# Attention scores in three PSUM banks with the context part shared, router results in the mixer bank, value products in three pieces

## The chip, the core and the metric

The program runs on one core of one Trainium2 chip. The time is that of the device, in microseconds (us), for one execution of the whole program. The engines of the core work in parallel, each through its own queue in order, and wait for each other through semaphores: TensorE (PE in the profile), VectorE (DVE), ScalarE (ACT), GpSimd (POOL) and SyncE (SP), which here only issues DMAs.

## What is computed

One layer of a hybrid backbone over 2048 tokens of width 1024, with 256 context tokens. The change lies in the part behind the input projection: windowed attention, the mixing of its rows with those of the Hyena branch, the output projection, the residual and the router. From the reference, cut:

```python
def block(i):                      # 16 blocks of 128 queries, 8 heads on 2 key heads
    qb = q[q0:q0+128]; kb = k_pad[q0:q0+384]; vb = v_pad[q0:q0+384]
    s_band = einsum('bqkgd,bskd->bkgqs', qb, kb) * ATT_SCALE     # 384 local keys, masked
    s_ctx  = einsum('bqkgd,bckd->bkgqc', qb, kc) * ATT_SCALE     # 256 context keys
    p = softmax(concatenate([s_sink, s_ctx, s_band], axis=-1))
    return p_ctx @ vc + p_band @ vb
...
mix = concatenate([rms_norm(att), rms_norm(hy)], axis=-1) @ w_out
x = x + g1 * mix
h = modulate(rms_norm(x, norm2_w), sh2, sc2)
# router: softmax over 4 groups, top 1; over its 8 experts, top 2; tokens sorted by expert
x = x + g2 * hierarchical_moe(h, ...)
```

## The kernel before

The program is a row of stages. Stages 1 to 4 make the modulation, the projection, the keys, queries and values, and the Hyena branch; stage 6 runs the experts. The change is in stage 5 (`stage5`), with one load in the stage ahead of it. Stage 5 goes over 16 tiles of 128 tokens (`NT = 16`) in a software pipeline (`pipeline`), steps -1 to 18. Step n of each engine's code holds five pieces of work, each for another tile:

- `scores`, tile n+1 (called `nx`): for each of 8 heads, TensorE multiplies the queries with the 256 context keys and the 384 local keys into PSUM. VectorE adds the mask, writes the sum to `pr` and takes the maximum, all in one instruction (`L2127`), then makes the bias (`L2131`). ScalarE takes the exponential (`L2040`).
- `values`, tile n: TensorE turns the exponentials by transposes (`L1932`, five groups of four for four heads, ten in all, into two alternating banks `PT`), ScalarE copies them out (`L2034`), TensorE multiplies them with the values into `OT` (`tile_values`, `L1956`, two halves of 10 products), turns the result (`turn_values`), and VectorE scales it into `mix`.
- `project`, tile n-1 (`pj`): TensorE transposes the normalised mixer rows into the two banks of `M` (`L1998`, semaphore `t1`), ScalarE and VectorE split them into a high and a low part (`L2087`, `L2213`, semaphore `t1v`), TensorE multiplies with `w_out` in two halves (`project_half`, `L1970` to `L1972`, 48 passes), VectorE adds the residual.
- `route`, tile n-2 (`ro`): ScalarE squares the new rows (`L2064`, semaphore `sq2`), GpSimd inverts the root (`n2d`), VectorE normalises them (`L2185`, `xnd`), TensorE transposes them into `M` (`L1980`, `t2`), VectorE and ScalarE scale them into `h2T` (`L2192`, `L2079`; `t2v`, `t2a`), TensorE makes the router's logits (`L2006`), VectorE picks group and experts in a chain of small instructions.
- `place`, tile n-3 (`pl`): GpSimd makes the one-hot picks (`L1860` to `L1863`, semaphore `picked`), TensorE sums them over the tokens (`L1988`, `L1989`), VectorE reads the sums (`L2207`), GpSimd works out the slots and scatters the records.

No scheduler sets the order: each engine's `step` is written out by hand, and the heads (`head(p)`) are the slots between which the other pieces stand. GpSimd's step begins with the wait for `sq2` of tile n-2, makes `n2d`, and only then makes the picks of tile n-3. SyncE's step n loads the queries of tile n+1 (`L1790`), waits for the normalised mixer rows and loads the Hyena rows of tile n+1 into `mix` (`L1796`), then loads the residual rows (`L1799`) and stores two results (`L1806`, `L1808`), each behind its wait. It goes to step n+1 only when it is through.

The eight PSUM banks are: `S` two (one head's scores, 640 columns, lie across both), `PT` two, `OT` one, `M` two, `R` one (router logits and pick sums). So the products of a head wait until VectorE has read those of the head before (semaphore `sm`); for tiles 0 and 1 odd heads use `M` and don't wait. The two products of a head use the two halves of TensorE's rows: the context keys rows 64 to 127, the local keys rows 0 to 63.

Of the kernel before, what the change touches and what calls it, by code (L numbers as in the profile page):

```python
# [1184 lines left out]
def stage4(e, g):  # L1185
# [24 lines left out]
    with e.stage() as st:  # L1210
# [50 lines left out]
        def _(sp):  # L1261
# [55 lines left out]
            sp.dma_start(g.mask[:, :, :], i["mask"].rearrange("p (a k) -> p a k", a=3)).then_inc(ld_att, 16)  # L1317
# [4 lines left out]
            sp.wait_ge(ld_att, 16 * 5)  # L1322
# [317 lines left out]
def stage5(e, g):  # L1640
# [3 lines left out]
    with e.stage() as st:  # L1644
# [3 lines left out]
        woh = e.sb(st, "woh", [P, KT, D], F32R)  # L1648
        rw = e.sb(st, "rw", [P, KT, NG + NE])
        rb = e.sb(st, "rb", [P, NG + NE])  # L1650
        g1 = e.sb(st, "g1row", [P, D])
        mask, sink = g.mask, g.sink
        e.sb(st, "mask_room", [P, 3, KEYS])
        e.sb(st, "sink_room", [P, NH])
        e.sb(st, "qb0_room", [2 * HD, NH, P])
# [19 lines left out]
        mixn = e.sb(st, "mixn", [P, 2, HW])  # L1675
# [18 lines left out]
        S = e.ps(st, "S", [P, 2 * 512])  # L1694
# [3 lines left out]
        R = e.ps(st, "R", [P, 512])  # L1698
# [68 lines left out]
        def score_banks(tile, p):  # L1767
            if tile.n < 2 and p % 2:
                return M[:, :, :].rearrange("p a b -> p (a b)")
            return S  # L1770

        @block.sync
        def _(sp):
            def step(t, scores, values, project, route, place):
# [9 lines left out]
                if scores:  # L1784
# [7 lines left out]
                    wait(sp, mxn, b.n - 1)  # L1792
                    if isinstance(b.n, int) and b.n == 0:
# [122 lines left out]
        def _(pe):  # L1916
            pe.wait_ge(setup, 6)

            def step(t, scores, values, project, route, place):
                nx, pj, ro, pl = t.back(-1), t.back(1), t.back(2), t.back(3)  # L1920

                def head(p):
# [12 lines left out]
                    if scores:  # L1935
                        if p == 0 and nx.n:
                            pe.wait_ge(ld_q[nx.par], 32 * (nx.half + nx.par))
                        wait(pe, sm, 8 * nx.n + p - (1 if nx.n < 2 and p >= 1 else 0))
                        h = order[p]
                        kv = h // 4  # L1940
                        to = score_banks(nx, p)
                        pe.matmul(to[:, 512 - C:512], qb[nx.par][HD:2 * HD, h, :], g.kT[HD:2 * HD, kv, 0:C],  # L1942
                                  start=True, stop=True)
                        pe.matmul(to[:, 512:512 + 3 * P], qb[nx.par][0:HD, h, :],  # L1944
                                  g.kT[0:HD, kv, bass.ds(nx.n * P, 3 * P)], start=True, stop=True).then_inc(qk, 1)

                def tile_values(half):
# [3 lines left out]
                    for a in range(5):  # L1951
                        for kv in range(2):
                            v = g.v[:, a, kv * HD:(kv + 1) * HD] if a < 2 else \
                                g.v[:, t.n + a, kv * HD:(kv + 1) * HD]
# [3 lines left out]
                    ins.then_inc(pv, 1)  # L1958
# [16 lines left out]
                for p in range(4):  # L1975
                    head(p)
                if route:
# [5 lines left out]
                if values:  # L1983
                    tile_values(0)
                head(4)
                if place:
                    pe.wait_ge(picked, pl.n + 1)
                    pe.matmul(R[:, 64:64 + NE], upper[:, :], pick[:, pl.par, 2, :], start=True, stop=True)  # L1988
                    pe.matmul(R[:, 128:128 + NE], ones[:, :].broadcast_to([P, P]), pick[:, pl.par, 2, :], start=True, stop=True).then_inc(px, 1)  # L1989
                for p in range(5, 7):  # L1990
                    head(p)
                if route:
                    pe.wait_ge(t2v, ro.n + 1)
                    pe.wait_ge(t2a, ro.n + 1)
                if project:
                    pe.wait_ge(mxn, pj.n + 1)
                    for k in range(KT):
                        ins = pe.transpose(M[:, k // 4, (k % 4) * P:(k % 4 + 1) * P],  # L1998
                                           mixn[:, k // 4, (k % 4) * P:(k % 4 + 1) * P], g.ident[:, :])
                    ins.then_inc(t1, 1)  # L2000
                head(7)
                if route:
                    if place:
                        pe.wait_ge(pxr, pl.n + 1)
                    for k in range(KT):
                        ins = pe.matmul(R[:, 0:NG + NE], h2T[:, k, :], rw[:, k, :], start=(k == 0), stop=(k == KT - 1))  # L2006
                    ins.then_inc(rt, 1)
# [15 lines left out]
        def _(act):  # L2023
            def step(t, scores, values, project, route, place):
# [71 lines left out]
                if values:  # L2096
# [4 lines left out]
                    act.activation(mixn[:, 0, :], mix[t.par][:, 0, :], ACT.Square, accum_out=ms[:, t.par, 0:1])  # L2101
                    act.activation(mixn[:, 1, :], mix[t.par][:, 1, :], ACT.Square, accum_out=ms[:, t.par, 1:2]).then_inc(sqa, 1)
# [3 lines left out]
        def _(ve):  # L2106
# [10 lines left out]
            def step(t, scores, values, project, route, place):  # L2117
                nx, pj, ro, pl = t.back(-1), t.back(1), t.back(2), t.back(3)

                def head(p):  # L2120
                    if scores:
                        edge = 1
                        if isinstance(nx.n, int):
# [3 lines left out]
                        ve.tensor_tensor_reduce(out=pr[:, p, :], in0=score_banks(nx, p)[:, 512 - C:512 + 3 * P],  # L2127
                                                in1=mask[:, edge, :], scale=1.0, scalar=-3e38, op0=ALU.add, op1=ALU.max,
# [52 lines left out]
                for p in range(3):  # L2181
                    head(p)
# [12 lines left out]
                if place:  # L2195
                    ve.wait_ge(px, pl.n + 1)
                    wait(ve, rec_ok, pl.n)
                if place and pl.n == NT - 1:
                    ve.wait_ge(based, 1)
                    ve.sem_inc(passed, 1)  # L2200
                    ve.tensor_copy(pxs[:, 1, :], R[:, 128:128 + NE]).then_inc(pxr, 1)
                    do(ve.tensor_tensor(pxs[:, 0, :], R[:, 64:64 + NE], base[:, :], ALU.add))
                    do(ve.tensor_tensor(pos[:, :, :], pick[:, pl.par, 0:2, :], pxs[:, 0:1, :].broadcast_to([P, 2, NE]), ALU.mult))
                    do(ve.tensor_reduce(out=selg[:, 0, 0:2], in_=pos[:, :, :], axis=AX.X, op=ALU.add))
                    ve.tensor_copy(idx[:, pl.par, :], selg[:, 0, 0:2]).then_inc(placed, 1)
                elif place:
                    ve.tensor_copy(pxs[:, :, :], R[:, 64:192].rearrange("p (a b) -> p a b", a=2)[:, :, 0:NE]).then_inc(pxr, 1)  # L2207
                head(5)
                head(6)
# [6 lines left out]
                if route:  # L2216
                    ve.wait_ge(rt, ro.n + 1)
                    wait(ve, rec_ok, ro.n - 1)
                    ve.tensor_tensor(lg[:, ro.par, :], R[:, 0:NG + NE], rb[:, :], ALU.add).then_inc(lgd, 1)
# [9 lines left out]
                if values:  # L2229
# [5 lines left out]
                    ve.wait_ge(ott, t.n + 1)  # L2235
                    ve.tensor_tensor(mix[t.par][:, 0, :].rearrange("p (k h d) -> p h k d", k=2, h=4),
# [584 lines left out]
```

## Time and profile before

| | us |
|---|---|
| median of 3 runs | 2511.38 |
| the runs | 2505.14, 2511.58, 2511.38 |
| the profiled execution | 2501.89 |
| its span | 2500.1 |
| TensorE busy in it | 2243.6 (90%) |
| VectorE, ScalarE, GpSimd busy | 1340.5, 1148.8, 504.6 |
| stage 5 in it | from about 1001 to about 1627 |

The profile page cuts the span into 40 slices with the busy tenths of each engine and the granted clock of TensorE. Slices 17 to 25 are the steady part of stage 5, in which one step follows the other at the same distance. The timeline gives each instruction with its start, its duration and, in brackets, how long its engine was idle before it and who released it. Matmuls are pipelined, so the duration of one includes its way through the array; the distance of two starts is what it costs.

### The profile page before, as it was taken

What the parts mean: (1) busy time and instruction counts of PE and PEld (TensorE: products, weight loads), DVE (VectorE), ACT (ScalarE), POOL (GpSimd) and SP (SyncE); (2) the same over time, 40 slices, a digit from 0 to 9 for tenths busy, and PEclk for the clock granted to TensorE, in tenths of its full rate; (3) what the DMA queues carried; (4) which work ended last, traced back from release to release, by engine and by line L of the source; (5) the groups of instructions that cost most, each with busy time, mean ns of one, the idle gap of its engine ahead of it and who ended that gap; (6) DMA issues with size and microseconds to landing.
All of it is one profiled execution on the core that took longest, in us unless ns stands there. A gap on an engine that the chain in (4) does not pass through costs nothing. (4 is left out here: it accounts for less than half of the span.)

```text
span 2500.1 us, 42870 instructions
## 1 busy us (share of the span) xinstructions
PE 2243.6 (90%) x15061; PEld 1535.7 (61%) x15062; DVE 1340.5 (54%) x2309; ACT 1148.8 (46%) x2065; POOL 504.6 (20%) x842
## 2 busy tenths in 40 slices
PE   5998999999989997799999999669899999898996
PEld 2336777888756665366666666546566666556664
DVE  4556784233245554555555554347556756455763
ACT  4666221222234442644554454146556656455653
POOL 2771110000011100002222222321222122222111
PEclk8999999999989998899999999679999999999999
DMA  8993223223473533421222121649888997777993
GB/s 305 310 259 95 55 55 97 61 58 92 106 184 88 139 88 95 124 68 52 72 77 72 47 73 56 217 158 318 281 264 290 332 318 246 244 231 248 334 305 103
DMA packets 241312, 413.61 MB, mean 165 GB/s; under 512 B 25555, under 2 KB 128859, under 8 KB 236115
## 3 DMA queue, kind: packets, MB, share of 16 engines
q1 hardware_dynamic: 197248, 353.84, 43.2%
q0 software_dynamic: 18800, 44.71, 7.7%
q10 hardware_dynamic: 25125, 13.18, 1.9%
q8 instruction: 90, 1.47, 0.3%
q14 instruction: 49, 0.40, 0.1%
HBM read 344.44 MB, written 76.85 MB: 169 GB/s over the span
## 5 line engine op out<-in xcount | busy, mean ns | idle before, releaser
L936 PE MATMUL ps_proj<-sb_hTh,sb_winh 128*128 128x512 f32 x576 | 234.0, 406 | 5.1 <-DVE sb_hTl L1088 2.4
L2692 PE MATMUL ps_byp<-sb_w,sb_gT 128*128 128x512 f32 x512 | 232.8, 597 | 1.1 <-ACT sb_gT L2499 1.1
L938 PE MATMUL ps_proj<-sb_hTh,sb_winl 128*128 128x512 f32 x576 | 225.0, 391 | 0.0
L937 PE MATMUL ps_proj<-sb_hTl,sb_winh 128*128 128x512 f32 x576 | 224.7, 390 | 0.0
L2127 DVE CUSTOM_DVE_ANT_0 sb_lead<-ps_S,sb_mask 128x640 f32<-128x640 f32 x120 | 98.7, 822 | 118.4 <-PE ps_S L1944 118.0
L2692 PEld LDWEIGHTS ps_byp<-sb_w,sb_gT 128*128 128x128 f32 x512 | 92.1, 190 | 94.7 <-issue 91.8
L2040 ACT ACTIVATE sb_lead<-sb_lead,sb_nm 128x640 f32<-128x640 f32 x128 | 106.2, 830 | 84.7 <-DVE sb_nm L2131 84.0
L2034 ACT COPY sb_lead<-ps_PT 128x512 f32<-128x512 f32 x160 | 89.3, 580 | 89.7 <-PE ps_PT L1932 89.7
L936 PEld LDWEIGHTS ps_proj<-sb_hTh,sb_winh 128*128 128x128 f32 x576 | 108.6, 189 | 33.4 <-issue 4.1
L1061 ACT COPY sb_rope_or_conv<-ps_proj 128x512 f32<-128x512 f32 x48 | 28.3, 589 | 219.1 <-PE ps_proj L938 144.6
L937 PEld LDWEIGHTS ps_proj<-sb_hTl,sb_winh 128*128 128x128 f32 x576 | 108.7, 189 | 25.6 <-issue 4.1
L938 PEld LDWEIGHTS ps_proj<-sb_hTh,sb_winl 128*128 128x128 f32 x576 | 108.4, 188 | 23.3
L1942 PE MATMUL ps_S<-sb_kT,sb_qb 64*128 64x256 f32 x240 | 85.4, 436 | 40.6 <-DVE sb_mx L2127 35.3
L2406 DVE TENSOR_TENSOR sb_w1l<-sb_raw,sb_w1h 128x1024 fp32r<-128x1024 f32 x64 | 74.1, 1220 | 87.5 <-ACT sb_w1h L2469 87.5
L2406 DVE TENSOR_TENSOR sb_w1l<-sb_lead,sb_w1h 128x1024 fp32r<-128x1024 f32 x64 | 74.0, 1220 | 84.2 <-ACT sb_w1h L2469 84.2
L2681 PE MATMUL ps_bh<-sb_w1h,sb_bxh 128*128 128x512 f32 x256 | 109.2, 426 | 8.7 <-DVE sb_bxl L2420 8.7
L1562 DVE TENSOR_TENSOR sb_ab<-sb_ab,ps_gp 128x1024 f32<-128x1024 f32 x64 | 75.3, 1218 | 70.9 <-PE ps_gp L1369 70.9
L1944 PE MATMUL ps_S<-sb_kT,sb_qb 64*128 64x384 f32 x240 | 111.6, 546 | 0.0
L2501 ACT ACTIVATE sb_sg<-ps_bh 128x512 f32<-128x512 f32 x32 | 19.2, 600 | 187.2 <-PE ps_bh L2681 181.0
L1970 PE MATMUL ps_M<-sb_woh,sb_mixh 128*128 128x512 f32 x256 | 104.9, 410 | 0.0
L1144 DVE TENSOR_SCALAR sb_rope_or_conv<-sb_rope_or_conv,sb_cols 128x2048 f32<-128x2048 f32 x11 | 14.8, 1346 | 163.8 <-ACT sb_rope_or_conv L1061 163.8
L1932 PEld LDWEIGHTS ps_PT<-sb_ident,sb_lead 128*128 128x128 f32 x640 | 71.1, 143 | 49.8 <-issue 44.7
(335 smaller groups left out, 5443.2 us busy)
## 6 DMA issues: line engine op xcount, KB each, us to landing
sb_lead<-in_exp_w SPq DMA_DIRECT2D x32, 2048.0 KB, 11.7
sb_w<-in_exp_w SPq DMA_DIRECT2D x32, 2048.0 KB, 9.0
sb_raw<-in_exp_w SPq DMA_DIRECT2D x32, 2048.0 KB, 12.1
sb_ada<-in_ada_w SPq DMA_DIRECT2D x16, 1536.0 KB, 7.7
scr_filt<-sb_fout SPq DMA_DIRECT2D x128, 128.0 KB, 3.3
sb_yh<-scr_filt SPq DMA_DIRECT2D x64, 256.0 KB, 5.1
scr_hy_in<-sb_hcT ACTq DMA_DIRECT2D x12, 1024.0 KB, 5.5
sb_win<-in_w_in SPq DMA_DIRECT2D x9, 1024.0 KB
```

Of the source, the lines that this page charges most:

```text
L936: pe.matmul(mp[:, r % 4, 0:N], a, high[:, k, :], start=(k == 0), stop=False)
L937: pe.matmul(mp[:, r % 4, 0:N], a, low[:, k, :], start=False, stop=False)
L938: ins = pe.matmul(mp[:, r % 4, 0:N], b, high[:, k, :], start=False, stop=(k == KT - 1))
L1942: pe.matmul(to[:, 512 - C:512], qb[nx.par][HD:2 * HD, h, :], g.kT[HD:2 * HD, kv, 0:C], start=True, stop=True)
L1944: pe.matmul(to[:, 512:512 + 3 * P], qb[nx.par][0:HD, h, :], g.kT[0:HD, kv, bass.ds(nx.n * P, 3 * P)], start=True, stop=True).then_inc(qk, 1)
L1970: pe.matmul(M[:, half, :], mixh[:, k, :], woh[:, k, cs], start=(k == 0), stop=False)
L2034: act.copy(pt[:, 4 * c:4 * c + 4, :].rearrange("p a t -> p (a t)"), PT[:, (t.par + c) % 2, :])\
L2040: act.activation(pr[:, p, :], pr[:, p, :], ACT.Exp, bias=nm[:, nx.par, p:p + 1], scale=SCALE, accum_out=rsum[:, nx.par, p:p + 1]).then_inc ...
L2127: ve.tensor_tensor_reduce(out=pr[:, p, :], in0=score_banks(nx, p)[:, 512 - C:512 + 3 * P], in1=mask[:, edge, :], scale=1.0, scalar=-3e38, ...
L2406: ve.tensor_tensor(piece(low[m], part), piece(raw13[par][:, m], part), piece(high[m], part).bitcast(F32), ALU.subtract).then_inc(lo[m], 1)
L2681: ins = pe.matmul(hp[:, m, :], a[:, k, :], b[m][:, k, :], start=(k == 0 and j == 0), stop=(k == KT - 1 and j == 2))
L2692: ins = pe.matmul(yp[:, part, :], gT[:, f, :], w2[par][:, f, part * 512:(part + 1) * 512], start=(f == 0), stop=(f == FT - 1), skip_group_ ...
```

## The change

1. `S` has three banks. An even head's local scores lie at the end of bank 0 and an odd head's at the start of bank 2; bank 1 holds the context scores of both, even ones in its first half, odd ones in its second. So each head's 640 columns are still in one piece, but local keys come first for even heads. The mask has 256 columns more, so that both orders can be cut from it, and is loaded in two DMAs; the value products take the chunks in the matching order.
2. TensorE's head p now issues the context product of head p, which alone raises `qk`, and behind it the local product of head p+1. Head 7 issues the local product of head 0 of the next tile, behind a wait for that tile's queries. Only tile 0 still uses `M` for odd heads.
3. `R` is now the first 128 columns of the second bank of `M`. The pick sums move on TensorE from behind head 4 to behind head 1, with waits for `picked` and for the residual `res`; their reading by VectorE moves from behind head 4 to behind head 1. The router's product moves from behind head 7 to ahead of head 6, VectorE's copy of the logits from behind head 7 to behind head 5, and TensorE waits for it (`lgd`) before it transposes the mixer rows.
4. The first half of the value products is cut in three: two chunks ahead of head 4, two behind it, the last behind head 6.
5. `mixn` is gone. The mixer rows are normalised in place in `mix`, and the squares go to `h2T`, behind a wait for `rt`. SyncE's load of the Hyena rows into `mix` therefore waits for `t1` (the transposes have read the rows) and stands at the end of its step.

The heart of the diff:

```diff
+            mask_of = [slice(C, KEYS + C), slice(0, KEYS)]
...
+            scores_of = [S[:, 512 - 3 * P:512 + C], S[:, 1024 - C:1024 + 3 * P]]
+            local_of = [S[:, 512 - 3 * P:512], S[:, 1024:1024 + 3 * P]]
+            context_of = [S[:, 512:512 + C], S[:, 1024 - C:1024]]
...
 (SyncE)
-                    wait(sp, mxn, b.n - 1)
...
-                    sp.dma_start(mix[b.par][:, 1, :], g.hyo_dram[bass.ds(b.n * P, P), :]).then_inc(ld_h[b.par], 16)
...
                     sp.wait_ge(xnd, b.n + 1)
                     sp.dma_start(g.xn_dram[bass.ds(b.n * P, P), :], xn[b.par][:, :]).then_inc(st_x[b.par], 16)
+                if scores:
+                    b = t.back(-1)
+                    wait(sp, t1, b.n - 1)
+                    sp.dma_start(mix[b.par][:, 1, :], g.hyo_dram[bass.ds(b.n * P, P), :]).then_inc(ld_h[b.par], 16)
...
 (TensorE)
+                def local(tile, p):
+                    if p == 0 and tile.n:
+                        pe.wait_ge(ld_q[tile.par], 32 * (tile.half + tile.par))
+                    return pe.matmul(mixer_local if tile.n == 0 and p % 2 else local_of[p % 2], qb[tile.par][0:HD, order[p], :],
+                                     g.kT[0:HD, order[p] // 4, bass.ds(tile.n * P, 3 * P)], start=True, stop=True)
...
+                        context.then_inc(qk, 1)
+                        if p + 1 == NH and nx.n + 1 < NT:
+                            wait(pe, sm, 8 * nx.n + p)
+                            local(nx.back(-1), 0)
+                        elif p + 1 < NH and not alone:
+                            local(nx, p + 1)
...
-                for p in range(4):
+                for p in range(2):
                     head(p)
+                if place:
+                    pe.wait_ge(picked, pl.n + 1)
+                    if route:
+                        pe.wait_ge(res, ro.n + 1)
+                    pe.matmul(R[:, 64:64 + NE], upper[:, :], pick[:, pl.par, 2, :], start=True, stop=True)
+                    pe.matmul(R[:, 96:96 + NE], ones[:, :].broadcast_to([P, P]), pick[:, pl.par, 2, :], start=True, stop=True).then_inc(px, 1)
+                for p in range(2, 4):
+                    head(p)
+                if place:
+                    pe.wait_ge(pxr, pl.n + 1)
...
                 if route:
                     pe.wait_ge(t2v, ro.n + 1)
                     pe.wait_ge(t2a, ro.n + 1)
+                    for k in range(KT):
+                        ins = pe.matmul(R[:, 0:NG + NE], h2T[:, k, :], rw[:, k, :], start=(k == 0), stop=(k == KT - 1))
+                    ins.then_inc(rt, 1)
...
                 if project:
+                    if route:
+                        pe.wait_ge(lgd, ro.n + 1)
                     pe.wait_ge(mxn, pj.n + 1)
```

How the instructions stand now. First TensorE in a steady step, before, from head 1 to the first values product (`ps_PT` is the turned exponentials, `ps_S` the scores, 256 columns for the context and 384 local):

```order
L1932 MATMUL ps_PT<-sb_ident,sb_lead 128x128 x4
L1942 MATMUL ps_S<-sb_kT,sb_qb 128x256
L1944 MATMUL ps_S<-sb_kT,sb_qb 128x384
L1932 MATMUL ps_PT<-sb_ident,sb_lead 128x128 x4
L1942 MATMUL ps_S<-sb_kT,sb_qb 128x256
L1944 MATMUL ps_S<-sb_kT,sb_qb 128x384
L1932 MATMUL ps_PT<-sb_ident,sb_lead 128x128 x4
L1942 MATMUL ps_S<-sb_kT,sb_qb 128x256
L1944 MATMUL ps_S<-sb_kT,sb_qb 128x384
L1980 MATMUL ps_M<-sb_ident,sb_xn_1 128x128 x8
L1956 MATMUL ps_OT<-sb_lead,sb_v 64x256 x10
```

The same engine and place after the change, where `L1948` is the context product of a head and `L1929` the local one of the next:

```order
L1948 MATMUL ps_S<-sb_kT,sb_qb 128x256
L1929 MATMUL ps_S<-sb_kT,sb_qb 128x384
L1994 MATMUL ps_M<-sb_pick,sb_upper 128x32
L1995 MATMUL ps_M<-sb_pick,sb_ones 128x32
L1942 MATMUL ps_PT<-sb_ident,sb_lead 128x128 x4
L1948 MATMUL ps_S<-sb_kT,sb_qb 128x256
L1929 MATMUL ps_S<-sb_kT,sb_qb 128x384
L1942 MATMUL ps_PT<-sb_ident,sb_lead 128x128 x4
L1948 MATMUL ps_S<-sb_kT,sb_qb 128x256
L1929 MATMUL ps_S<-sb_kT,sb_qb 128x384
L2003 MATMUL ps_M<-sb_ident,sb_xn_0 128x128 x8
L1968 MATMUL ps_OT<-sb_lead,sb_v 64x256 x4
```

The pick sums now stand between head 1 and head 2, and only four of the ten products of the first values half stand behind the transposes. Then TensorE at the end of the heads, before:

```order
L1998 MATMUL ps_M<-sb_ident,sb_mixn 128x128 x8
L1932 MATMUL ps_PT<-sb_ident,sb_lead 128x128 x4
L1942 MATMUL ps_S<-sb_kT,sb_qb 128x256
L1944 MATMUL ps_S<-sb_kT,sb_qb 128x384
L2006 MATMUL ps_R<-sb_rw,sb_h2T 128x36 x8
L1956 MATMUL ps_OT<-sb_lead,sb_v 64x256 x10
L1970 MATMUL ps_M<-sb_woh,sb_mixh 128x512
```

And after, where the last `L1929` is that of the next tile:

```order
L2016 MATMUL ps_M<-sb_rw,sb_h2T 128x36 x8
L1942 MATMUL ps_PT<-sb_ident,sb_lead 128x128 x4
L1948 MATMUL ps_S<-sb_kT,sb_qb 128x256
L1929 MATMUL ps_S<-sb_kT,sb_qb 128x384
L1968 MATMUL ps_OT<-sb_lead,sb_v 64x256 x2
L2028 MATMUL ps_M<-sb_ident,sb_mix 128x128 x8
L1942 MATMUL ps_PT<-sb_ident,sb_lead 128x128 x4
L1948 MATMUL ps_S<-sb_kT,sb_qb 128x256
L1929 MATMUL ps_S<-sb_kT,sb_qb 128x384
L1968 MATMUL ps_OT<-sb_lead,sb_v 64x256 x10
L1983 MATMUL ps_M<-sb_woh,sb_mixh 128x512
```

The router's product went ahead of the mixer's transposes. Last SyncE's queue, one round of it, before:

```order
L1808 DMA scr_xn<-sb_xn_0 128x1024
L1790 DMA sb_qb<-scr_q 64x1024 x2
L1796 DMA sb_mix<-scr_hy_out 128x512
L1799 DMA sb_xres<-in_x 128x1024
L1806 DMA out<-sb_x_1 128x1024
```

And after:

```order
L1808 DMA scr_xn<-sb_xn_0 128x1024
L1812 DMA sb_mix<-scr_hy_out 128x512
L1792 DMA sb_qb<-scr_q 64x1024 x2
L1799 DMA sb_xres<-in_x 128x1024
L1806 DMA out<-sb_x_1 128x1024
```

The load of the Hyena rows, which waits for `t1`, now stands ahead of the two loads of queries.

## Rows read from the trace of the kernel before

**Rows 1.** The page: span, and granted clock of TensorE in 40 slices

```profile
span 2500.1 us, 42870 instructions
...
PEclk8999999999989998899999999679999999999999
```

**Rows 2.** Timeline of TensorE in step 8: start, duration, line, output from inputs, idle

```profile
1294.05 0.48 PE L1942 MATMUL ps_S<-sb_kT,sb_qb 64*128 64x256 f32 x1
...
1296.04 0.48 PE L1942 MATMUL ps_S<-sb_kT,sb_qb 64*128 64x256 f32 x1 [0.49 <-DVE sb_mx L2127]
...
1296.36 0.38 PE L1942 MATMUL ps_S<-sb_kT,sb_qb 64*128 64x256 f32 x1
1296.47 0.48 PE L1944 MATMUL ps_S<-sb_kT,sb_qb 64*128 64x384 f32 x1
1296.89 0.66 PE L1932 MATMUL ps_PT<-sb_ident,sb_lead 128*128 128x128 f32 x4
...
1300.94 1.09 PE L1980 MATMUL ps_M<-sb_ident,sb_xn 128*128 128x128 f32 x8
...
1305.29 0.48 PE L1942 MATMUL ps_S<-sb_kT,sb_qb 64*128 64x256 f32 x1
...
1310.53 1.09 PE L1998 MATMUL ps_M<-sb_ident,sb_mixn 128*128 128x128 f32 x8
...
1312.83 1.98 PE L2006 MATMUL ps_R<-sb_rw,sb_h2T 128*128 128x36 f32 x16
1314.74 2.38 PE L1956 MATMUL ps_OT<-sb_lead,sb_v 128*64 128x256 f32 x20
1317.05 0.51 PE L1970 MATMUL ps_M<-sb_woh,sb_mixh 128*128 128x512 f32 x1
```

**Rows 3.** Timeline of VectorE, step 8, head 0

```profile
1295.15 0.82 DVE L2127 CUSTOM_DVE_ANT_0 sb_lead<-ps_S,sb_mask 128x640 f32<-128x640 f32 x1 [0.35 <-PE ps_S L1944]
```

**Rows 4.** Waits from 1044 to 1550: us in total, times, longest

```profile
PE ps_S L1942 <- DVE sb_mx L2127: 34.5, 56, 1.8
```

**Rows 5.** Timeline of GpSimd, step 8: root of the norm, and last pick instruction

```profile
1296.18 0.19 POOL L1846 TENSOR_SCALAR sb_n<-sb_n 128x1 f32<-128x1 f32 x1 [5.06 <-ACT sb_xn L2064]
...
1299.01 0.25 POOL L1863 TENSOR_TENSOR sb_pick<-sb_pick 128x32 f32<-128x32 f32 x1 [0.17 <-POOL sb_pick L1860]
```

**Rows 6.** Timeline of ScalarE, step 8: exponential of head 4, scaling of half of h2T

```profile
1307.52 0.83 ACT L2040 ACTIVATE sb_lead<-sb_lead,sb_nm 128x640 f32<-128x640 f32 x1 [1.48 <-DVE sb_nm L2131]
...
1308.72 1.48 ACT L2079 ACTIVATE sb_h2T<-ps_M,sb_mods,sb_scale 128x128 f32<-128x128 f32 x4
```

**Rows 7.** Timeline of SyncE's queue, steps 8 and 9: start and duration of the issue

```profile
1292.06 0.33 SPq L1796 DMA_DIRECT2D sb_mix<-scr_hy_out  x1
...
1301.27 1.26 SPq L1790 DMA_DIRECT2D sb_qb<-scr_q  x2
1327.62 0.33 SPq L1796 DMA_DIRECT2D sb_mix<-scr_hy_out  x1
```

**Rows 8.** DMA issues from 1160 to 1520: count, size, median us to landing

```profile
sb_qb<-scr_q SPq DMA_DIRECT2D x18, 256.0 KB, 4.5
sb_mix<-scr_hy_out SPq DMA_DIRECT2D x10, 256.0 KB, 2.6
```

**Rows 9.** TensorE by stretch: length, busy (instructions), granted clock, DMA share, GB/s

```profile
1042.00:1046.00 4.00, 1.89 (x10) 0.95 0.23 57
1046.00:1056.00 10.00, 9.90 (x39) 0.51 0.34 108
...
1294.00:1298.00 4.00, 3.05 (x18) 1.00 0.56 113
```

**Rows 10.** Timeline of TensorE in step 1, at the low clock

```profile
1046.73 0.79 PE L1942 MATMUL ps_S<-sb_kT,sb_qb 64*128 64x256 f32 x1
...
1049.45 0.79 PE L1942 MATMUL ps_S<-sb_kT,sb_qb 64*128 64x256 f32 x1
...
1051.13 4.53 PE L1956 MATMUL ps_OT<-sb_lead,sb_v 128*64 128x256 f32 x20
```

More of the change, by code:

```diff
@@ L1935, in head, with tile_values @@
                     if scores:
[L1936 to L1947, printed above, removed]
+                        alone = nx.n == 0
+                        wait(pe, sm, 8 * nx.n + p - (1 if alone else 0))
+                        context = pe.matmul(mixer_context if alone and p % 2 else context_of[p % 2], qb[nx.par][HD:2 * HD, order[p], :],
+                                            g.kT[HD:2 * HD, order[p] // 4, 0:C], start=True, stop=True)
+                        if alone:
+                            context = local(nx, p)
+                        context.then_inc(qk, 1)
[4 more added lines that the diff above has]
+                            local(nx, p + 1)
+                def tile_values(half, chunks=range(5)):
                     pe.wait_ge(tc, 10 * t.n + 5 * half + 5)
@@ L1983, in step @@
                 if values:
-                    tile_values(0)
+                    tile_values(0, range(0, 2))
                 head(4)
[L1986 to L1991, printed above, removed]
+                if values:
+                    tile_values(0, range(2, 4))
+                head(5)
                 if route:
@@ L1998, in step @@
                         ins = pe.transpose(M[:, k // 4, (k % 4) * P:(k % 4 + 1) * P],
-                                           mixn[:, k // 4, (k % 4) * P:(k % 4 + 1) * P], g.ident[:, :])
+                                           mix[pj.par][:, k // 4, (k % 4) * P:(k % 4 + 1) * P], g.ident[:, :])
                     ins.then_inc(t1, 1)
                 head(7)
[L2002 to L2007, printed above, removed]
                 if values:
@@ L2180, in step @@
                     residual(ro, 1).then_inc(res, 1)
[L2181 to L2182 removed]
+                head(0)
+                head(1)
+                if place:
+                    ve.wait_ge(px, pl.n + 1)
+                    wait(ve, rec_ok, pl.n)
+                if place and pl.n == NT - 1:
+                    ve.wait_ge(based, 1)
+                    ve.sem_inc(passed, 1)
+                    ve.tensor_copy(pxs[:, 1, :], R[:, 96:96 + NE]).then_inc(pxr, 1)
+                    do(ve.tensor_tensor(pxs[:, 0, :], R[:, 64:64 + NE], base[:, :], ALU.add))
+                    do(ve.tensor_tensor(pos[:, :, :], pick[:, pl.par, 0:2, :], pxs[:, 0:1, :].broadcast_to([P, 2, NE]), ALU.mult))
+                    do(ve.tensor_reduce(out=selg[:, 0, 0:2], in_=pos[:, :, :], axis=AX.X, op=ALU.add))
+                    ve.tensor_copy(idx[:, pl.par, :], selg[:, 0, 0:2]).then_inc(placed, 1)
+                elif place:
+                    ve.tensor_copy(pxs[:, :, :], R[:, 64:64 + 2 * NE].rearrange("p (a b) -> p a b", a=2)).then_inc(pxr, 1)
+                head(2)
                 if route:
@@ L2194, in step @@
                     ins.then_inc(t2v, 1)
[L2195 to L2207, printed above, removed]
                 head(5)
+                if route:
+                    ve.wait_ge(rt, ro.n + 1)
+                    wait(ve, rec_ok, ro.n - 1)
+                    ve.tensor_tensor(lg[:, ro.par, :], R[:, 0:NG + NE], rb[:, :], ALU.add).then_inc(lgd, 1)
                 head(6)
```

67 lines of the change are left out of this document (35 added, 32 removed).

## The prediction

> **What bounds the kernel now.** I read the page first, then the timeline of one steady step of stage 5, engine by engine, and the waits. Stage 5 is a quarter of the span of 2500.1 us [rows 1]; nothing outside it changes but one mask load. SyncE's load of the Hyena rows comes at 1292.06 and again at 1327.62 [rows 7], so a steady step takes 35.56 us. TensorE sets that length: it idles about 2.4 us in a step, nearly all of it before scores products that wait for VectorE, 34.5 us in 56 waits over 14 steps [rows 4]. I number the heads 0 to 7 and call the four transposes (of turned exponentials) and the two score products of a head its work.
>
> The loop of one head is seen in two timelines [rows 2, 3]. The products start at 1294.05, VectorE at 1295.15 (1.10 later), the next products at 1296.04 (0.89 after VectorE started); heads follow at 1.99 us. Two products cost 0.85 us (1296.04 to 1296.89) and the transposes of a head 0.5, so 1.35 us is work and the rest waiting. The two products run side by side: the second pass of the context product ends at 1296.74, that of the local product at 1296.95 [rows 2].
>
> **Part by part.**
>
> *Scores.* VectorE will wait for the context product alone, which ends 0.21 us sooner; the next local product runs beside it at no cost. The loop shrinks from 1.99 to 1.78 us. The value pieces fill waits behind heads 4 and 5. All idle time of TensorE, 2.4 us a step, is the ceiling of this gain.
>
> *Pick sums behind head 1: a new wait.* Before, they stood behind head 4 (after 1305.3), and the picks had long been ready. GpSimd makes the last pick instruction at 1299.01, ending 1299.26 [rows 5]. It can't come earlier, since GpSimd first waits for ScalarE's squares of the new residual (released at 1296.18) [rows 5], and that chain starts with VectorE's residual of this same step; none of it is changed. TensorE is through head 1 at 1296.04 - 0.21 + 0.85 = 1296.7. It stands 2.65 us with heads 2 to 7 queued behind it, and VectorE, which waits for the sums behind its own head 1, stands too. This is work moved ahead of its producer.
>
> *From there to the mixer's transposes*, at the full clock: sums 0.5 (4 of the short passes of which 16 take 1.9 [rows 2]) to 1299.85; heads 2 and 3 with one wait of 0.43 to 1303.0; transposes of the rows 1.0; 8 of 20 value passes 0.95; eight transposes 1.0; head 4's products start at 1306.0. The router's product, now ahead of head 6, needs h2T. ScalarE ends it at 1308.72 + 1.48 = 1310.2 [rows 6], which is 4.9 us after head 4's products began (1305.29); less the 0.21, that is 1310.7. TensorE is there at 1309.15 (products 0.85, values 0.95, head 5 1.35) and waits 1.55 us. This wait too is new: before, the router stood behind head 7, at 1312.83. Router 1.9, head 6 1.35, last 4 value passes 0.45: the mixer's transposes begin at 1314.4, where they began at 1310.53 [rows 2]. That is 3.9 us later, 1.9 of it the router's product, which before came behind them.
>
> *The next tile's local product: a second new wait.* SyncE's queue now holds, in order, the wait for `t1`, the load of the Hyena rows, and the two loads of queries of tile n+2. Before, the queries were issued at 1301.27 with 28 us to spare. Now they go out after `t1` of step n, and step n's head 7 asks for them directly behind `t1`. `t1` comes at 1315.5. The Hyena rows take 0.4 to issue and the second query load starts 0.55 later. If it lands like the Hyena rows (2.6), that is 3.6 after `t1`; if like the query loads of before (4.5, with a 512 KB store just ahead of them) [rows 8], 5.5. I take 4.2, since only 256 KB go ahead. TensorE resumes at 1319.7; local product 0.75, the 20 value passes 2.3 [rows 2], and the projection starts at 1322.8 instead of 1317.05: 5.75 us a step. The Trainium skill ("DMA: Bandwidth & Descriptors", section on the anatomy of one DMA) fits a DMA by 2.0 us plus bytes over 436 GB/s; for the 768 KB in flight it would give 3.8 after the first issue, about 0.4 less than my value, some 5 us in all. Without this wait, ScalarE's last copy (exponential 6, mixer split, copy) would let the values begin at about 1317.6 and the projection at 1319.9: 2.85 us a step from the other waits alone.
>
> The wait for `lgd`, the squares into `h2T` and the normalising in place find their inputs ready; they cost nothing. The 384 KB more of mask lands under the Hyena stage. Behind the projection's start nothing changes, VectorE's picking chain ends before its next input.
>
> *The clock.* From 1042 to 1046 TensorE was busy 1.89 of 4.00 us, after which the granted clock was 0.51 for 10 us, though it was busy 9.90 of them [rows 9]; at 0.5, that is 1.2 GHz instead of 2.4. From 1294 to 1298 it is busy 3.05 of 4.00 and the clock stays at 1.00. With 2.65 us of standing, the four microseconds around the picks hold about 1.2 busy, less than the stretch that cost the clock. At 1.2 GHz the heads of step 1, without a gap between them, did not bring it back, the long values product (4.53 us for 20 passes, from 1051.13) did [rows 10]. The change cuts just that product in pieces of 8, 8 and 4 passes among heads and transposes, so I expect the low clock to last to the second half of the values. The Trainium skill ("TensorE: Matmul & The Clock Gate", section on HAM oscillation) tells of a loop whose short groups of matmuls are parted by DMA waits and which is put back to the low clock in every pass; by that rule the fall here would come in each step too.
>
> Its price: two heads at the low clock start 2.72 apart (1046.73, 1049.45) [rows 10], twice the work of 1.35. From 1299.35: sums 0.9, heads 2 and 3 5.4, transposes 1.8, values 4.2 in all, head 4 with its eight transposes 3.8, heads 5 and 6 5.4, router 3.6, mixer's transposes 1.8, together 26.9, and `t1` at 1326.2 (h2T is then ready in time). Plus 4.2 for the queries, 1.3 for the local product, 4.1 values and 0.5 of slow projection: 1336.3, which is 19 us a step more. Bounds for this term: 5.75 (clock holds) and 19. I take six steps in seven as falling and the rest at 7.8 (only the second wait costs the clock): 17.4.
>
> **The sum.** Steps 3 to 13 have both waits: 11 x 17.4 = 191. Step 14 has no next tile to load: 14. Step 2 has no picks: 5. Step 1: 4. Step 15 (no scores, picks wait at the low clock): 10. Step 16, where the router's product no longer hides the splitting of the mixer rows: 5. Step 17: 2.5. Others 1. Together 232. No later stage absorbs it, since the experts start from the last records. On the profiled execution's 2501.9 us that is 2734; the median of the runs is 9 us above that execution, which gives 2743. I say 2735.
>
> **Rivals.** *The clock holds* through both waits: 11 x 5.75 + 19 for the other steps = 82, so 2584 to 2593. For it: the new gaps are 2.65 and 3.3 us amid busy stretches. Against: the stretch from 1042. *The clock comes back midway*, behind the first value pieces: about 12 us a step, 2670. *Only the queries' wait binds* (picks ready earlier than I read): mixer transposes at 1311.8, 5.5 us a step with its slow values, 2575. *Only the picks' wait binds* (queries land under head 7): 16 us a step, 2700. *Faster*: neither wait binds and h2T too is ready. The place is head 1, the price 2.65 us; it turns only if GpSimd's picks end before 1296.7 instead of 1299.26. Then the heads keep their shorter loop, 1.5 us a step are gained over 13 steps, 20 us: 2490. If only h2T binds, the projection starts at 1317.2 against 1317.05 and nothing is gained. *Worse than my sum*: the projection too runs slow for long, over 2775.
>
> **Chances.** Forecast 0.45 (its own range 2690 to 2775), clock back midway 0.15, clock holds 0.14, queries alone 0.08, picks alone 0.07, neither 0.05 (faster 0.03, same 0.02), worse 0.06. A measurement of this kernel tells about 0.3% from no change. Faster 0.03, same 0.02, slower 0.95. The range from 2585 to 2770 leaves out the last two, most of queries alone and a little of both ends.
>
> **What would show it.** A steady step of 50 to 55 us by the distance of the Hyena loads. TensorE idle 2.6 us before the pick sums, released by GpSimd; 2 to 3.5 us before the local product behind head 7, released by the query load; the granted clock of stage 5's slices at 6 or 7 instead of 9. Head loop 1.78 us where the clock is full. If the first wait is missing, my reading of GpSimd's order is wrong; if the second, that of SyncE's; if both are there and the clock is 1.00, the step takes 41.3 us.

## The result, and the profile after

| | before | after |
|---|---|---|
| median (4 runs each, side by side), us | 2511.48 | 2732.27 |
| the runs, us | 2505.14 to 2513.89 | 2726.78 to 2741.18 |
| the profiled execution, us | 2501.89 | 2734.64 |
| steady step of stage 5, us | 35.56 [rows 7] | 52.8 (mean of ten, 51.1 to 56.9) |

The ratio is 1.089, with a 95% interval from 1.087 to 1.091: 221 us slower, where the prediction said 2735 us. The page of the changed kernel, its lines for span, busy time and granted clock, to be held against [rows 1]:

```profile
span 2732.8 us, 42960 instructions
...
PE 2369.2 (87%) x15061; PEld 1596.0 (58%) x15062; DVE 1343.4 (49%) x2309; ACT 1152.8 (42%) x2065; POOL 504.2 (18%) x842
...
PEclk8999999999899989888878777867999999999999
```

TensorE is busy 126 us longer (2243.6 before) with the same 15061 matmuls, since many run slower: the slices of stage 5 show a granted clock of 7 and 8 (and 6 once, near its end), where the steady ones showed 9. SyncE's queue gives the distance of two steps, 53.29 us, and the new order of its loads:

```profile
1310.60 0.32 SPq L1812 DMA_DIRECT2D sb_mix<-scr_hy_out  x1
...
1363.89 0.32 SPq L1812 DMA_DIRECT2D sb_mix<-scr_hy_out  x1
1364.26 1.09 SPq L1792 DMA_DIRECT2D sb_qb<-scr_q  x2
```

Next TensorE's timeline of one step of the changed kernel, step 7, from its head 0 (1335.24) to the next (1389.00); it answers to [rows 2]. At 53.8 us it is one of the longer steps. Where a duration is near twice that of its neighbour of the same shape, the clock is low:

```profile
1337.98 0.48 PE L1948 MATMUL ps_S<-sb_kT,sb_qb 64*128 64x256 f32 x1 [0.27 <-DVE sb_mx L2154]
...
1341.47 0.41 PE L1994 MATMUL ps_M<-sb_pick,sb_upper 128*128 128x32 f32 x2 [2.58 <-POOL sb_pick L1867]
...
1344.63 0.79 PE L1948 MATMUL ps_S<-sb_kT,sb_qb 64*128 64x256 f32 x1
...
1346.22 1.97 PE L2003 MATMUL ps_M<-sb_ident,sb_xn 128*128 128x128 f32 x8
...
1348.12 1.93 PE L1968 MATMUL ps_OT<-sb_lead,sb_v 128*64 128x256 f32 x8
1349.98 1.09 PE L1942 MATMUL ps_PT<-sb_ident,sb_lead 128*128 128x128 f32 x8
...
1355.83 2.80 PE L2016 MATMUL ps_M<-sb_rw,sb_h2T 128*128 128x36 f32 x16 [1.46 <-ACT sb_h2T L2103]
...
1362.09 1.77 PE L2028 MATMUL ps_M<-sb_ident,sb_mix 128*128 128x128 f32 x8
...
1371.63 1.62 PE L1929 MATMUL ps_S<-sb_kT,sb_qb 64*128 64x384 f32 x2 [6.71 <-DMA sb_qb<-scr_q]
1373.18 4.34 PE L1968 MATMUL ps_OT<-sb_lead,sb_v 128*64 128x256 f32 x20
...
1377.44 0.50 PE L1983 MATMUL ps_M<-sb_woh,sb_mixh 128*128 128x512 f32 x1
```

The three new waits are those of the prediction: for the picks 2.58 us, for `h2T` 1.46, for the queries 6.71 (4.4 to 8.0 in the steps 3 to 12). The one for `h2T` the prediction had only for a full clock; with the clock low it took it to vanish. Two heads follow at 1.78 us (1336.20 to 1337.98). TensorE by stretches of that step (length, busy time, granted clock, DMA share, GB/s) shows that the clock does not stay low from the first wait on, but falls and comes back three times:

```profile
1337.00:1341.00 4.00, 1.62 (x9) 1.00 0.68 185
...
1342.00:1346.00 4.00, 4.00 (x17) 0.63 0.02 5
1346.00:1349.00 3.00, 3.00 (x13) 0.50 0.43 173
1349.00:1352.00 3.00, 3.00 (x20) 0.85 0.00 0
1352.00:1356.00 4.00, 2.54 (x18) 1.00 0.00 2
1356.00:1360.00 4.00, 4.00 (x22) 0.59 0.00 0
1360.00:1363.00 3.00, 3.00 (x13) 0.50 0.01 3
...
1366.00:1372.00 6.00, 0.37 (x1) 0.58 0.50 116
1372.00:1379.00 7.00, 7.00 (x29) 0.63 0.01 2
1379.00:1389.00 10.00, 10.00 (x47) 1.00 0.00 0
```

In windows of half a microsecond between 1080 and 1500 I counted the stretches with a granted clock under 0.75: none before, 23 with 163 us in sum after, about three in each step. The same count is given below for each experiment. In the step shown they are 1343.0 to 1350.0, 1356.5 to 1363.5 and 1367.0 to 1377.0: the first two begin 1.5 and 0.7 us after TensorE has resumed work, the third begins 2 us into the wait for the queries. The lag is not the same in every step: in the six others of the count that wait for picks, the clock falls already within that wait.

### The profile page after: what moved, and what is told of

Same layout as the page of the kernel before. It is cut to its first block and busy times, and to the rows that moved or that the text cites. A ratio compares the mean times of both kernels' runs of the same rounds, so it can differ in the third digit from the quotient of the medians.

```text
span 2732.8 us, 42960 instructions
## 1 busy us (share of the span) xinstructions
PE 2369.2 (87%) x15061; PEld 1596.0 (58%) x15062; DVE 1343.4 (49%) x2309; ACT 1152.8 (42%) x2065; POOL 504.2 (18%) x842
## 5 line engine op out<-in xcount | busy, mean ns | idle before, releaser
L1929 PE MATMUL ps_S<-sb_kT,sb_qb 64*128 64x384 f32 x248 | 149.2, 691 | 74.5 <-DMA sb_qb<-scr_q 74.4
L1968 PE MATMUL ps_OT<-sb_lead,sb_v 128*64 128x256 f32 x640 | 118.2, 517 | 5.0 <-ACT sb_lead L2058 5.0
L1948 PE MATMUL ps_S<-sb_kT,sb_qb 64*128 64x256 f32 x248 | 109.8, 531 | 13.4 <-DVE sb_mx L2154 8.7
L1942 PE MATMUL ps_PT<-sb_ident,sb_lead 128*128 128x128 f32 x640 | 115.7, 320 | 1.2 <-ACT sb_lead L2058 0.7
L1942 PEld LDWEIGHTS ps_PT<-sb_ident,sb_lead 128*128 128x128 f32 x640 | 87.4, 168 | 43.8 <-issue 37.5
```

The source lines that it names most:

```text
L1929: return pe.matmul(mixer_local if tile.n == 0 and p % 2 else local_of[p % 2], qb[tile.par][0:HD, order[p], :], g.kT[0:HD, order[p] // 4, b ...
L1942: ins = pe.transpose(PT[:, (t.par + c) % 2, a * P:(a + 1) * P], pr[:, at // 5, (at % 5) * P:(at % 5 + 1) * P], g.ident[:, :])
L1948: context = pe.matmul(mixer_context if alone and p % 2 else context_of[p % 2], qb[nx.par][HD:2 * HD, order[p], :], g.kT[HD:2 * HD, order[p ...
L1968: ins = pe.matmul(OT[kv * HD:(kv + 1) * HD, half, :, :], v, x, start=(a == 0), stop=(a == 4), skip_group_check=True)
```

## The experiments

My theory: three steps of TensorE were moved ahead of their producers (picks, `h2T`, queries), and each new wait costs itself and a fall of the clock to its lower level (0.50, 1.2 GHz) for some 7 us. The rivals: the clock is lost for another reason (the short pieces of work among the heads), so that the waits alone are worth little; or the cut of the value products keeps it low, as the prediction said. All kernels are the changed one with the edit that is shown; each time is a median, and ratios are against runs of the kernel before beside it.

| kernel | us | ratio, 95% interval | low stretches, us in them |
|---|---|---|---|
| before | 2506.6 to 2512.2 | 1 | 0, 0 |
| changed | 2732.3 | 1.087 to 1.091 | 23, 163 |
| picks first | 2644.2 | 1.050 to 1.060 | 15, 112 |
| queries first | 2620.0 | 1.042 to 1.049 | 17, 130 |
| both | 2539.0 | 1.011 to 1.016 | 9, 63 |
| scatters late | 2708.2 | 1.077 to 1.084 | 23, 165 |
| picks wait filled | 2699.5 | 1.072 to 1.077 | 14, 101 |
| both, `h2T` wait filled | 2509.7 | 0.998 to 1.002 | 0, 0 |
| both, `h2T` early | 2488.8 | 0.990 to 0.993 | 0, 0 |
| `h2T` early alone | 2657.1 | 1.056 to 1.061 | 17, 122 |
| values uncut | 2752.6 | 1.092 to 1.098 | 23, 177 |
| both, `h2T` early, uncut | 2502.2 | 0.995 to 0.998 | 0, 0 |

**Picks first.** GpSimd makes the picks of tile n-3 before it waits for the squares of tile n-2:

```diff
 (GpSimd, step)
-                if route:
-                    b = t.back(2)
-                    pool.wait_ge(sq2, b.n + 1)
...
                     pool.tensor_tensor(pick[:, b, 2, :], pick[:, b, 0, :], pick[:, b, 1, :], ALU.add).then_inc(picked, 1)
+                if route:
+                    b = t.back(2)
+                    pool.wait_ge(sq2, b.n + 1)
```

> The changed kernel, but GpSimd makes the picks of tile n-3 ahead of its wait for the squares of tile n-2, so they are ready before TensorE is through head 1. Theory (two waits behind a producer, each of which also costs the clock): the 2.6 us wait before the pick sums goes, and with it the low stretch of the clock behind it (about 3 us of work in 6.8 us); the router's wait and the query wait stay. About 5 us a step less, 12 steps: 2660 to 2685. Rival (the pick wait is only covered by something else late at the same point, such as the row normalisation): under 15 us less, 2715 or more. Rival (the shared context bank or the cut value product is itself the cost): no change, 2725 to 2740.

2644.15 us (2635.74 to 2652.57, 2 runs). The wait went, and 88 us with it, 16 more than the better end of what was expected. The count goes with that: 15 low stretches in 420 us, so about 1.7 are left in a step of 46.4 us (mean of eleven steps), not two. The wait for `h2T` is still there in each step, 1.46 us long, but not each of them is followed by a low stretch any more.

**Queries first.** SyncE issues the queries of tile n+2 as soon as head 7 has read the old ones, ahead of its wait for `t1`; they no longer stand behind the Hyena rows:

```diff
 (SyncE, step, in front of the Hyena rows)
+                    b, c = t.back(-1), t.back(-2)
+                    if 2 <= c.n < NT:
+                        sp.wait_ge(qk, 8 * (c.n - 1))
+                        (the two loads of queries of tile c)
                     wait(sp, t1, b.n - 1)
```

> The changed kernel, but SyncE issues the queries of tile n+2 ahead of its wait for t1, so they land 20 us before head 7 asks for them; the Hyena rows stay where they are. Theory: the 5.7 to 7.5 us wait before the next tile's local product goes in 13 steps, and about 2.5 us of slow values and projection behind it: 8 to 10 us a step less, 2605 to 2630. Rival (ScalarE's last copy takes the wait's place, as worked out for the case without it): at least 3 us of it stay, 2640 to 2670. Rival (no part of the loss is the queries): over 2715.

2619.98 us (2618.11 to 2621.85, 2 runs): as expected. 112 us hang on the order of two entries in SyncE's queue.

**Both.**

> Both edits together. Theory: only the router's wait for h2T (1.5 us) is left of the new waits, the shorter head loop pays it back, the clock stays at 1.00 in the steady steps: 2500 to 2525, step 35.3 to 36.3 us. Rival (placing the router's product ahead of head 6 and waiting for the logits costs by itself): 2535 to 2570. Rival (the three-bank scores bring the gain that they promise once the waits are gone): 2475 to 2495.

2538.96 us (2537.51 to 2545.24, 4 runs). The theory is missed by 14 us and the time lies in the first rival's range: the clock did not stay at 1.00. Of the 221 us, 193 are gone. Whether it is the place of the router's product or its wait that costs the rest is settled further down, in the run with this wait filled. TensorE's timeline of this kernel:

```profile
1360.37 3.16 PE L2023 MATMUL ps_M<-sb_rw,sb_h2T 128*128 128x36 f32 x16 [1.46 <-ACT sb_h2T L2110]
```

After 1.46 us without work the router's product takes 3.16 us, where its 16 short passes took 1.98 [rows 2]. That step is 39.3 us long. The wait of 1.46 us does not always take the clock with it: of ten such waits between 1100 and 1500, nine have a low stretch behind them (3 to 10 us long) and one has none. Its product runs at the full clock, and its step takes 35.56 us:

```profile
1207.61 1.95 PE L2023 MATMUL ps_M<-sb_rw,sb_h2T 128*128 128x36 f32 x16 [1.46 <-ACT sb_h2T L2110]
```

What sets this one apart is not known.

**Scatters late.** The query loads landed later than predicted. GpSimd's scatters of the records (128 small ones each) are issued just ahead of them; here they wait for the first half of the projection:

```diff
 (GpSimd, ahead of the two scatters)
+                    if project:
+                        pool.wait_ge(op, 2 * t.back(1).n + 1)
```

> The changed kernel, but GpSimd's scatter of the records waits until the first half of the projection is done, so that its small packets no longer go out just ahead of the Hyena rows and the queries. Theory (the scatters slow the loads): the query loads land in 3.5 to 4.5 us as before instead of 5.2 to 8.5, 2 to 3.5 us a step less: 2690 to 2710. Rival (the loads are slow for another reason, such as their order on the queue or the Hyena rows ahead of them): landings stay at 5 to 8 us, 2725 to 2740.

2708.15 us (2706.11 to 2710.19, 2 runs). The loads land sooner: 3.9 instead of 5.9 us for the queries, 2.6 instead of 4.8 for the Hyena rows. From SyncE's release by `t1` to the local product 4.95 us pass (1312.84 to 1317.79) instead of 7.74 (1363.89 to 1371.63), and the number of low stretches is the same. The scatters themselves are small: 448 packets with 0.02 MB in the seven steps from 1150 to 1500. DMA issues of the changed kernel, and behind them those of this one (count, size, median us to landing):

```profile
sb_qb<-scr_q SPq DMA_DIRECT2D x14, 256.0 KB, 5.9
sb_mix<-scr_hy_out SPq DMA_DIRECT2D x7, 256.0 KB, 4.8
```

```profile
sb_qb<-scr_q SPq DMA_DIRECT2D x14, 256.0 KB, 3.9
sb_mix<-scr_hy_out SPq DMA_DIRECT2D x7, 256.0 KB, 2.6
```

**Picks wait filled.** The clock's price by itself: the wait stays, but TensorE has work while it lasts.

```diff
 (TensorE, behind head 1)
+                if place and scores:
+                    for _r in range(4):
+                        local(nx, 2)
                 if place:
                     pe.wait_ge(picked, pl.n + 1)
```

> The changed kernel with the wait for the picks kept, but TensorE fed while it lasts: ahead of it four repeats of the local product of head 2, with the same result (about 2.6 to 3 us, as long as the wait of 2.58). If the clock falls because the engine stands there, one of the three low stretches of 6.8 us a step goes, and with it about 3 us a step, less 0.3 for the filler: 2700 to 2712, with the clock full from head 2 to the first values and 8 low stretches fewer. Rival: the clock does not hang on this wait, and the time stays at 2732 to 2740 with as many low stretches as before.

2699.49 us (2693.77 to 2702.75, 3 runs): 33 us less though nothing useful was added, and 9 low stretches fewer. Over the 12 steps that have the filler, the clock behind this wait costs some 3 us a step, as much as the wait.

**Both, `h2T` wait filled.** The same test at the third wait, with two repeats of `local(nx, 6)` ahead of the router's waits:

> The kernel with picks and queries first (2539 us), with two repeats of the local product of head 6 ahead of the router's wait for h2T, with the same result (about 1.5 us, as long as the wait of 1.46). The wait itself is kept, only TensorE does not stand in it. If the fall of the clock is its price, the router product takes 1.9 us instead of 3.16, the steps with a low stretch lose it, about 3 to 4 us a step: 2495 to 2510. Rival: the clock falls all the same, since short products with 36 columns and transposes are too little for it, and the time is 2535 to 2545.

2509.65 us (2501.67 to 2523.37, 10 runs), no low stretch left, a step of 35.8 us. In its timeline the wait has shrunk to 0.17 us and the product is back at the full clock:

```profile
1340.52 1.95 PE L2026 MATMUL ps_M<-sb_rw,sb_h2T 128*128 128x36 f32 x16 [0.17 <-ACT sb_h2T L2113]
```

So neither the place of the router's product nor the short products and transposes around it lose the clock. Without the idle time of 1.46 us at that place it stays.

**Both, `h2T` early.** On ScalarE and VectorE the scaling into `h2T` moves from behind head 4 to ahead of it:

```diff
 (ScalarE; the same on VectorE)
                 head(3)
+                (wait for t2, four scalings into h2T, t2a)
                 head(4)
                 if place:
...
-                (wait for t2, four scalings into h2T, t2a)
                 head(5)
```

> The kernel with picks and queries first (2539 us), with the scaling into h2T ahead of head 4 on ScalarE and VectorE, where both stand idle (0.8 and 2.95 us), so that the router's product finds its input. If the wait of 1.46 us and the clock behind it are what is left, a step loses 1.46, 1.2 on the router and about 3 on the heads behind: from 39.2 to 33.5 to 35 us, 2470 to 2500, faster than the kernel before by the shorter head loop. Rival: something else gives way (the logits wait, copies of the turned exponentials delayed by h2T, or the clock falling elsewhere), and the time stays over 2506.

2488.77 us (2484.66 to 2495.59, 6 runs), faster than the kernel before by 0.85%, interval 0.7% to 1.0%. Its steps are 34.30 us long:

```profile
1303.16 0.33 SPq L1817 DMA_DIRECT2D sb_mix<-scr_hy_out  x1
1337.46 0.33 SPq L1817 DMA_DIRECT2D sb_mix<-scr_hy_out  x1
```

That is the gain that the change holds, 1.26 us a step against 35.56, once its three orders are put right: 23 us in all. No run makes the same three moves in the kernel before, so it is not shown that all of it needs the third bank. For it speaks that from 1080 to 1500 the only TensorE waits which the profile of the kernel before lists are those for VectorE ahead of scores (29.4 us).

**`h2T` early alone**, on the changed kernel:

> The changed kernel with the scaling into h2T ahead of head 4, and nothing else. One of the three waits of a step goes (1.46 us) with its low stretch (about 3 us), so about 4 us over 13 steps: 2675 to 2695. Rival: with the clock low from the picks on, h2T is in time for the slow heads anyway or the next wait takes it over, and the time is 2715 to 2735.

2657.07 us (2655.67 to 2662.78, 3 runs): 75 us less, more than the 37 to 57 expected. The step taken away was worth one wait and one low stretch, as planned; what came on top is the query wait, which fell from 5.9 us (mean of steps 3 to 12 of the changed kernel; 6.71 in the step shown) to 4.1 to 4.5. `t1` is now raised before GpSimd scatters, as the trace shows: SyncE issues at 1385.30, GpSimd only at 1387.33.

```profile
1385.30 0.32 SPq L1812 DMA_DIRECT2D sb_mix<-scr_hy_out  x1
1385.66 1.09 SPq L1792 DMA_DIRECT2D sb_qb<-scr_q  x2
```

```profile
1387.33 1.14 POOL L1905 DMA_INDIRECT scr_table<-sb_rec,sb_idx  x1 [0.90 <-POOL sb_idx L1901]
```

In the changed kernel the order is the other way round, and the loads behind the scatters (issued at 1363.89 and 1364.26, above) are the slow ones:

```profile
1361.21 1.14 POOL L1905 DMA_INDIRECT scr_table<-sb_rec,sb_idx  x1 [0.89 <-POOL sb_idx L1901]
1362.65 0.98 POOL L1905 DMA_INDIRECT scr_table<-sb_rec,sb_idx  x1 [0.30 <-issue]
```

The query loads of this kernel land in 4.0 us, the Hyena rows in 2.8. This is a second path to the same finding, without a touch on the scatters.

**Values uncut.** The first half of the value products in one piece ahead of head 4 again, on the changed kernel:

```diff
                 if values:
-                    tile_values(0, range(0, 2))
+                    tile_values(0)
                 head(4)
...
-                    tile_values(0, range(2, 4))
...
-                    tile_values(0, range(4, 5))
```

> The changed kernel with the first half of the value products in one piece of 20 passes ahead of head 4, as before the change; all else is kept, the three waits too. The prediction said that the long values product brings the clock back and that cutting it keeps the clock low from the picks to the second half. By that step the clock would come back sooner now and the time would fall to 2690 to 2715. Rival: the clock comes back in any case some 7 us after it fell, cut or not, and the time is 2725 to 2745, or up to 15 us more since nothing stands in the waits behind heads 4 and 5.

2752.60 us (2735.78 to 2756.45, 4 runs): 20 us more, some 5 beyond the end of the rival's range, and 23 low stretches as before the edit. The clock does not come back sooner with the long product: the low stretch at the picks is 6.5 or 7 us long in both kernels, but for one of 10 in the uncut one. The rival holds, and the step of the prediction by which the cut keeps the clock low is refuted. Part of the 20 us is the wait for `h2T`, which lasts 2.14 us here instead of 1.46.

**The same cut, where the clock is full**, on the kernel of 2488.8 us:

> The kernel with picks, queries and h2T ahead of their readers (2488.8 us), with the first half of the value products in one piece. It prices the cut where the clock stays full. If the pieces fill waits of TensorE behind heads 4 and 5 (their waits for VectorE and ScalarE), these come back: 0.3 to 1 us a step, 2493 to 2502. Rival: the pieces fill nothing, as the head loop there is bound by VectorE only in 0.27 us a head, and the time stays within 3 us.

2502.17 us (2491.09 to 2505.84, 11 runs). Its steps are 34.95 us long, 0.65 more, which over 13 steps is 8 us of the 13. By this the cut is worth half of what the repaired change gains in a step.

## Why the prediction came out right

The total was met within 3 us, but two of its terms were wrong in opposite directions. The times of step 7, counted from its head 0 (1335.24; in the step that the prediction worked from, 1293.08), against those that it forecast:

| from head 0 to | forecast, us | measured, us |
|---|---|---|
| pick sums | 6.3 | 6.2 |
| `t1` | 33.1 | 28.7 |
| local product of the next tile | 37.3 | 36.4 |
| projection | 43.2 | 42.2 |
| next head 0 | 54.8 | 53.8 |

- **The head loop**: 1.78 us, as forecast. The ceiling of this gain was named rightly as TensorE's idle time of 2.4 us; 1.26 a step were got when nothing else stood in the way. The rival "faster" had 1.5 us a step and 2490 for that case; with the three moves it is 2488.8.
- **The picks' wait**: 2.58 us against 2.65, released by GpSimd. The reasoning by order, that GpSimd makes them behind a wait whose chain begins in the same step, carried over, and moving the picks took the wait away.
- **The wait for `h2T`**: 1.46 against 1.55. Right, but the prediction took it to vanish behind a low clock (26.9 us from picks to `t1`). In fact the clock was back by then, so this wait exists, and a second low stretch stands behind it.
- **The clock from picks to `t1`**: the term that was too large. Forecast were 26.9 us all at the low level; 22.4 passed (1341.47 to 1363.89), and only 21.0 in seven of the steps 3 to 13. The failing step is that only a long values product brings the clock back. In the trace it comes back some 8.4 us after the pick sums began: the first 8 value passes still take 1.93 us, and head 4's eight transposes right behind them 1.09, their time at the full clock. In the six other steps of the count it is back 5.5 to 5.9 us after the pick sums began. The uncut kernel is no better. This was the rival "back midway" for this term.
- **The queries' wait**: the term that was too small. From `t1` to the local product 7.74 us passed (6.4 to 9.5 in the steps 3 to 12), forecast were 4.2 with bounds of 3.6 and 5.5; the 2 to 3.5 us of idle time that the prediction wanted to see there are 4.4 to 8.0. Order and place were right. The price was bounded by rows of loads with no scatter just ahead of them [rows 8]; that GpSimd's scatters would come to lie just ahead of these loads was not looked at. Without them it is 4.95 and 5.09 us in two kernels, still inside the bounds. The estimate of 3.8 us from the fit in the Trainium skill ("DMA: Bandwidth & Descriptors", section on the anatomy of one DMA) is below all of these; that section is about DMAs which GpSimd issues, these go through SyncE's queue.
- **The steps in sum**: 232 us were summed, 232.7 is the difference between the two spans. From the mixer's transposes of step 3 to those of step 14, eleven steps, 391.4 us pass before (1132.41 to 1523.83) and 583.2 after (1154.78 to 1737.93): 191.7 more, where 11 x 17.4 = 191 was used. The rest, 41 us at both ends, agrees as well, but was not looked into step by step.

How close the total came is luck. The 17.4 us a step were 19 for six steps in seven and 7.8 for the seventh; in fact steady steps cost 17.2 on average, and none came near 7.8 (the shortest took 51.1 us, 15.6 more than before). Too much low clock behind the picks, too little wait for the queries and the share of steps without a fall, of which there were none, happened to cancel. And the sum on the median would have been 2743, 11 us above the measured time; the 2735 that the prediction names stand 8 us below it without a reason given. What was right for its reasons is that the two main waits come, where, behind whom, and that they take the clock with them.

Each wait costs 75 to 112 us when it alone is taken away, 275 in sum, where taking all three away gives 244: the three overlap little. A wait is dear here since it is paid twice, once as idle time and once as clock. For the picks the filler gives back 33 us, which is the clock. Taking the wait away gives 88; of the 55 between them 12 waits of 2.58 us are 31, and the rest is not taken apart (with picks first the wait is gone in the last steps too, where the filler does not run). In the Trainium skill ("TensorE: Matmul & The Clock Gate", the section on a second failure mode) a kernel is told of in which short idle times between groups of matmuls let the clock go back and forth; the trace here agrees, with pauses of 1.46 and 2.58 us and a granted clock of 0.50 behind them. The section on oscillation, which the prediction used, is about waits for DMAs of some 3 to 5 us; here the release came from GpSimd or ScalarE in two cases of three, after shorter waits, so that the falls behind these two do not follow from it.

## What to carry to other kernels

Before a step is moved ahead in an in-order queue, look up for each of its inputs when the last producer ends, in the timeline of that producer's engine, and move the producer's piece first if it stands behind an unrelated wait; here three such moves turned 221 us of loss into 23 of gain. A pause of 1.5 us in a TensorE that is otherwise full can cost as much again in clock, which a run with harmless repeated work in the pause tells from the wait itself. When a transfer lands late, look at what every other queue has issued just ahead of it.

## What was not expected of the hardware

- Two indirect stores of 128 small records each, issued 1.2 and 2.7 us ahead, made 256 KB loads land in 4.8 instead of 2.6 us (Hyena rows) and in 5.9 instead of 3.9 us (queries). Shown by two kernels that changed the order in different ways. Whether it is the number of the packets, their writes, or where they go in memory stays open.
- Behind a pause of 1.46 us the granted clock fell from 1.00 to 0.50 nine times out of ten; with the pause at 0.17 us, at the same place, it stayed at 1.00. In the kernel before, the waits of TensorE from 1080 to 1500 (total, times, longest) were these, and there was no low stretch among them:

```profile
PE ps_S L1942 <- DVE sb_mx L2127: 29.4, 49, 0.9
```

So 49 pauses of up to 0.9 us did no harm, and one of 1.46 a step did in most steps. It does not hang on the length of the pause alone, since the same pause in the same kernel once did nothing (and twice in picks first, at 1143.19 and 1330.43); what else it hangs on stays open.
- The low stretches of the changed kernel lasted 7 us on average (163 us in 23): 21 of them 6.5 or 7.0 us, two 10.0, whether long value products stood behind the pause or heads and transposes. In the other kernels some lasted only 3 or 3.5.
